# Paged attention of a decoder step: page gathers gated apart, transposes inside the scores, four slots of turned pages

## The chip, the cores and the metric

One Trainium2 chip, of which the program uses one core. The metric is the device time of one execution in microseconds (us). The kernel before takes 3054.34 us, the median of three runs (3053.44 to 3055.99).

## What is computed

The program runs two layers of a decoder on 1024 prompt tokens and on 8 sequences of 8 new tokens. The change touches one stage of the first layer: attention of the new tokens over a cache of pages. Each of the 8 sequences has 64 pages of 128 cached tokens, in an order that a table gives; a cached token is a latent row of 256 numbers (ckv) and a rotary row of 32 (kpe). All in float32.

```python
def mla_scores(q_lat, q_pe, ckv, kpe):
    s = jnp.einsum('bhsr,btr->bhst', q_lat, ckv) + jnp.einsum('bhsk,btk->bhst', q_pe, kpe)
    return s.astype(jnp.float32) * SCALE_B

def online_update(carry, sc, v):
    m, l, acc = carry
    m_new = jnp.maximum(m, jnp.max(sc, axis=-1))
    alpha = jnp.exp(m - m_new)
    p = jnp.exp(sc - m_new[..., None])
    l_new = l * alpha + jnp.sum(p, axis=-1)
    acc_new = acc * alpha[..., None] + jnp.einsum('bhst,btr->bhsr', p, v.astype(jnp.float32))
    return (m_new, l_new, acc_new)

    def page_step(carry, pages):          # of paged_attend
        ck = cache_ckv[layer, pages]
        kp = cache_kpe[layer, pages]
        return online_update(carry, mla_scores(q_lat, q_pe, ck, kp), ck), None
```

## The kernel before

The stage (stage_paged) takes the sequences in four pairs. A pair's tokens are read in 8 units, so there are H = 32 units, which this text calls periods: period h is the work on unit h. One unit is two gathers of 1 MiB, one for each sequence of the pair (e = 0, 1; 128 rows of 8 KB, one row to a partition), and holds two groups g = 2h and 2h + 1 of 4 tokens in each partition. Five sets of buffers hold gathered pages. The rotary rows come in gathers of 256 KB, one for each sequence and two units. All these gathers are issued by GpSimd (gather_pages, L2691; gather_kpe, L2697). Before unit h may be gathered, GpSimd waits until the scores of h - 3 are finished (`scored`) and until the old pages of its set were used (`valued`). It then issues e = 0, e = 1, and in every even period both rotary gathers behind them.

VectorE turns each group by 32x32 blocks (turn_pages, L2701, two of 128x1024 a group; turn_kpe, L2704, two of 128x128) into cT and kT, which have three slots; group g + 3 may only be turned when the scores that read group g are over.

TensorE does for each period, in this order:

- turn_p(h - 1), L3177: 8 transposes of the probabilities of the period before, 128x128, into two PSUM banks;
- scores(h), L3165: 72 matmuls on 32x64 parts of the array (8 chunks of 32 latent numbers and one chunk of rotary numbers, 8 matmuls each), 256 columns, into PSUM S_;
- values(h - 1), L3193: 16 matmuls of 128x64, the turned probabilities by the pages.

In the trace a float32 matmul of scores or values stands as two instructions (144 and 32 a period), a transpose as one (8), and each has a weight load beside it: 184 MATMUL and 184 LDWEIGHTS a period.

After scores(h) VectorE takes the maximum (L3289, L3291, L3293), ScalarE takes the exponential (L3249, L3252), which overwrites the probabilities `pr` and so waits for turn_p(h - 1), and later copies the turned probabilities out of PSUM (copy_p, L3243), for which values(h - 1) waits. VectorE's list for period h is: maxes(h), turn(2h + 3), sums(h - 1) (L3300, L3304), turn(2h + 4). All semaphores and the order on each engine are written out by hand. scores(h) waits for both turned groups, for both turned rotary groups and for the exponential of h - 1 (S_ is one buffer).

SyncE loads the queries of the next pair three times in the stage (load_rows, L2710).

Of the kernel before, what the change touches and what calls it, by code (L numbers as in the profile page):

```python
# [21 lines left out]
F32 = mybir.dt.float32  # L22
# [4 lines left out]
P = 128  # L27
# [9 lines left out]
NH, NOPE, ROPE, VD = 8, 64, 32, 64  # L37
QR, KR = 384, 256
# [2614 lines left out]
class FirstPages:  # L2653
# [3 lines left out]
    def __init__(self, c, cm):  # L2657
        nc = c.nc
        n = 2 * G4 * KR
        self.second = tile(nc, cm, "pages_ckv0", [P, 2 * G4, KR])  # L2660
        raw = nc.alloc_sbuf_tensor_at(f"pages_first_{nc.next_id()}", [P, 2 * G4, KR], F32, offset=c.raw_at)
        self.queries = tile(nc, cm, "q_all", [P, NH * T])
        self.units = [[raw[:, :, :], self.second[:, :, :]]]
        self.units += [[self.queries[:, (2 * u + e) * n:(2 * u + e + 1) * n].rearrange("p (j r) -> p j r", r=KR) for e in range(2)]
                       for u in range(2)]
        self.kpe = tile(nc, cm, "pages_kpe0", [P, 2, NG // NQK, G4 * ROPE])
        m = NG // NQK * G4 * ROPE
        self.later_kpe = self.queries[:, 4 * n:4 * n + m].rearrange("p (a d) -> p a d", a=NG // NQK)
        self.q_rows = tile(nc, cm, "q_rows0", [P, KR // 32 + 1, 2, NH * NT])
        self.keys = tile(nc, cm, "k_all", [P, NH * NPR])  # L2670
        self.own_m = tile(nc, cm, "own_max", [P, NPAIR])
        self.own_b = tile(nc, cm, "own_bias", [P, NPAIR])
        self.sums = tile(nc, cm, "sum_all", [P, NPAIR])
        self.units_in = [nc.alloc_semaphore(f"pages_in{u}") for u in range(2)]
        self.kpe_in = nc.alloc_semaphore("first_kpe_in")
        self.q_in = nc.alloc_semaphore("first_q_in")
        self.turned = nc.alloc_semaphore("pages_turned")
        self.kturned = nc.alloc_semaphore("kpe_turned")
        self.sems = [*self.units_in, self.kpe_in, self.q_in, self.turned, self.kturned]
        n = 3 * 2 * G4 * KR  # L2680
        self.cT = self.keys[:, 0:n].rearrange("p (s e j r) -> p s e j r", s=3, e=2, j=G4)
        m = n + 3 * 2 * G4 * ROPE
        self.kT = self.keys[:, n:m].rearrange("p (s e j r) -> p s e j r", s=3, e=2, j=G4)
        self.later_rows = self.keys[:, m:m + (KR // 32 + 1) * 2 * NH * NT].rearrange("p (n e r) -> p n e r", e=2, r=NH * NT)
# [15 lines left out]
    def turn_pages(self, dve, g, e, src):  # L2700
        return dve.transpose(self.cT[:, g % 3, e, :, :].rearrange("p j r -> p (j r)"), src.rearrange("p j r -> p (j r)"))  # L2701

    def turn_kpe(self, dve, g, e, src):
        return dve.transpose(self.kT[:, g % 3, e, :, :].rearrange("p j r -> p (j r)"), src[e][:, g % (NG // NQK), :])  # L2704

# [347 lines left out]
def stage_paged(c, ckv, ctok, qlat, qpe, yb, ring, w_next, first):  # L3053
# [10 lines left out]
    W = 2 * G4 * P  # L3064
    NCH = KR // 32
    with Stage(nc) as cm:
        last = tile(nc, cm, "pages_ckv1", [P, 2, 2 * G4, KR])
        spare = nc.alloc_sbuf_tensor_at(f"pages_ckv2_{nc.next_id()}", [P, 2, 2 * G4, KR], F32, offset=c.ring_at + 4 * 4 * KD * P)
        units = first.units + [[t[:, e, :, :] for e in range(2)] for t in (last, spare)]
        pk = [[first.kpe[:, 0, :, :], first.kpe[:, 1, :, :]],  # L3070
              [first.later_kpe, tile(nc, cm, "pages_kpe1", [P, NG // NQK, G4 * ROPE])[:, :, :]]]
        cT, kT = first.cT, first.kT
        q9 = [first.q_rows, first.later_rows]
# [4 lines left out]
        ls, own_m = first.sums, first.own_m  # L3078
        wkv = cT[:, 0, :, :, :].rearrange("p e j r -> p (e j r)").rearrange("p (k n) -> p k n", k=2)
        olat = pr.rearrange("p (k h b t) -> p k h b t", k=2, h=NH, b=NB)  # L3080
# [8 lines left out]
        wkv_in, = sems(nc, cm, "wkv_in")  # L3089
        pt_half, = sems(nc, cm, "pt_half")  # L3090
        (own_turned, own_copied, own_valued, own_ready,
# [38 lines left out]
        def _(pool):  # L3130
            for h in range(2, H):
                if h >= 3:
                    pool.wait_ge(scored, h - 2)
                if h >= NSETS:
                    pool.wait_ge(valued, 2 * (h - NSETS) + 2)
                for e in range(2):
                    first.gather_pages(pool, c, units[h % NSETS][e], h, e, p_in[h % NSETS])
                if h % 2 == 0:
                    v = h // 2
                    if v >= 2:  # L3140
                        pool.wait_ge(kturned, (v - 1) * (NG // NQK))
                    for e in range(2):
                        first.gather_kpe(pool, c, pk[v % 2][e], v, e, k_in[v % 2])
# [6 lines left out]
        def _(pe):  # L3150
            def scores(h):
                i = h // NH_
                lo, hi = sorted((2 * h % 3, (2 * h + 1) % 3))
                pair = slice(lo, hi + 1, hi - lo)
                pe.wait_ge(q_in[i % 2], 272 * (i // 2) + 272)
                pe.wait_ge(turned, 2 * h + 2)
                pe.wait_ge(kturned, 2 * h + 2)
                if h >= 1:
                    pe.wait_ge(exped, h)
                for n in range(NCH + 1):  # L3160
                    for a in range(4):
                        rows = slice(32 * a, 32 * a + 32)
                        for e in range(2):
                            keys = cT[rows, pair, e, :, 32 * n:32 * n + 32] if n < NCH else kT[rows, pair, e, :, :]
                            ins = pe.matmul(S_[64 * e:64 * e + 64, a, :].rearrange("p (s j i) -> p s j i", s=2, j=G4),  # L3165
                                            q9[i % 2][rows, n, e, :], keys, start=(n == 0), stop=(n == NCH))
                ins.then_inc(scored, 1)

# [11 lines left out]
            def values(h):  # L3180
# [8 lines left out]
                for j in range(2 * G4):  # L3189
                    g = 2 * h + j // G4  # L3190
                    m = P * (j if 2 * h % 3 < (2 * h + 1) % 3 else (j + G4) % (2 * G4))
                    for e in range(2):
# [14 lines left out]
            for h in range(1, H):  # L3207
                turn_p(h - 1)
                scores(h)
                values(h - 1)  # L3210
# [58 lines left out]
        def _(dve):  # L3269
            def turn(g):  # L3270
                v = g // (NG // NQK)
                if g >= 3:
                    dve.wait_ge(scored, (g - 3) // 2 + 1)
                if g % 2 == 0:
# [31 lines left out]

            turn(2)
            for h in range(H):
                maxes(h)
                if 2 * h + 3 < G:  # L3310
                    turn(2 * h + 3)
                if h == 0:
                    dve.wait_ge(own_valued, 1)
                    for i in range(NPAIR):
                        ins = dve.tensor_copy(acc[:, i, :], ownO[i])
                    ins.then_inc(own_ready, 1)
                else:
                    sums(h - 1)
                if 2 * h + 4 < G:
                    turn(2 * h + 4)  # L3320
            def normalise(lo, hi, done):
# [947 lines left out]
```

## Time and profile before

| what | value |
|---|---|
| median of the runs | 3054.34 us (3053.44 to 3055.99, n = 3) |
| the profiled execution, its own time | 3060.39 us |
| its span | 3058.6 us, 1.8 us less than its time |
| mean granted TensorE clock | 0.967 |
| busy share of TensorE, VectorE, ScalarE, GpSimd | 93%, 57%, 35%, 40% |
| the paged stage, first scores to last values | about 603 to 950 us of the span |

A line of the lists by group gives the busy time in us, then the mean ns of one, then the idle time of the engine just before instructions of the group with what ended it; "issue" is an engine that waited for nothing that the profile shows. A line of the windows gives first the window and its length; the first of them runs from the exponential of period 0 to that of period 31, the others are single periods. A timeline line gives start and duration in us, engine, source line, operation, tiles and shapes, a count where neighbours are merged, and in brackets the idle time before it.

### The profile page before, as it was taken

Reading aid. Unit: us, or ns where it says so; the run is one execution under the profiler, and the core shown is the slowest. Engines: PE = TensorE matmul, PEld = TensorE weight load, DVE = VectorE, ACT = ScalarE, POOL = GpSimd, SP = SyncE. Lnnn points to the kernel's source line nnn. Section 1 sums busy time; section 2 is a strip of 40 time slices with the busy share of each in tenths; the row PEclk is TensorE's granted clock in tenths of the full one; section 3 lists DMA queues with packets and bytes.
Section 4 is the critical chain, followed back from the end, with each engine's and each line's share of the span. In section 5 each row is a group of like instructions: output and inputs, shape, how many; then the busy total and the mean of one; then the engine's idle time right before and its main releaser. Section 6 shows DMA issues by size and latency. Waiting matters only on the chain. (4 is left out here: it accounts for less than half of the span.)

```text
span 3058.6 us, 60317 instructions
## 1 busy us (share of the span) xinstructions
PE 2833.5 (93%) x24873; PEld 2580.9 (84%) x24873; DVE 1741.8 (57%) x3025; ACT 1080.1 (35%) x2174; POOL 1214.7 (40%) x835
## 2 busy tenths in 40 slices
PE   6999899888987989999999997987998999999996
PEld 4888676566666989999999986977998999999996
DVE  5331245566765586666653256888387666664234
ACT  5511026522223553333321034765453333331112
POOL 2411147622223544444433134875544444443202
PEclk8999989999998999999999998999999999999998
DMA  9555300166663322232265232201432232346422
GB/s 313 174 194 191 116 22 1 60 226 229 233 222 94 102 80 100 89 111 99 102 230 186 73 123 76 65 17 31 120 96 85 87 113 88 114 159 214 144 81 81
DMA packets 232380, 377.88 MB, mean 124 GB/s; under 512 B 14506, under 2 KB 155179, under 8 KB 223652
## 3 DMA queue, kind: packets, MB, share of 16 engines
q1 hardware_dynamic: 200092, 253.95, 25.3%
q0 software_dynamic: 11776, 75.50, 6.8%
q10 hardware_dynamic: 20240, 44.57, 4.0%
q8 instruction: 199, 3.26, 0.4%
q14 instruction: 73, 0.60, 0.1%
HBM read 298.71 MB, written 73.28 MB: 122 GB/s over the span
## 5 line engine op out<-in xcount | busy, mean ns | idle before, releaser
L796 PE MATMUL ps<-HS,w_split 128*128 128x272 f32 x1920 | 272.2, 292 | 22.6 <-ACT sg L1053 10.3
L796 PEld LDWEIGHTS ps<-HS,w_split 128*128 128x128 f32 x1920 | 252.9, 190 | 28.3 <-ACT sg L1053 15.0
L812 PE MATMUL ps<-HS,w_ring 128*128 128x272 f32 x1920 | 273.0, 288 | 0.0
L812 PEld LDWEIGHTS ps<-HS,w_ring 128*128 128x128 f32 x1920 | 253.7, 189 | 0.0
L2317 PEld LDWEIGHTS ps<-HS_in,w_split 128*128 128x128 f32 x1728 | 222.6, 191 | 27.7 <-issue 16.4
L2317 PE MATMUL ps<-HS_in,w_split 128*128 128x272 f32 x1728 | 233.4, 294 | 9.2 <-DVE HS_in L2536 9.1
L1791 DVE TENSOR_TENSOR Y<-Y,ps 128x272 f32<-128x272 f32 x256 | 112.2, 438 | 224.6 <-PE ps L812 224.6
L1389 POOL TENSOR_TENSOR w_split<-w_raw,w_split 128x512 fp32r<-128x512 f32 x120 | 170.5, 1433 | 156.0 <-ACT w_split L1045 156.0
L767 PE MATMUL ps<-HS,w_ring 128*128 128x272 f32 x1344 | 179.0, 294 | 22.3 <-PEq L161 12.1
L767 PEld LDWEIGHTS ps<-HS,w_ring 128*128 128x128 f32 x1344 | 174.6, 192 | 24.9 <-POOLq L1438 12.3
L1389 POOL TENSOR_TENSOR w_ring<-w_raw,w_ring 128x512 fp32r<-128x512 f32 x40 | 61.6, 1539 | 269.9 <-ACT w_ring L1045 269.9
L3564 PE MATMUL ps<-HS,w_ring 128*128 128x272 f32 x1032 | 139.5, 298 | 14.6 <-ACT Y L3738 9.0
L3564 PEld LDWEIGHTS ps<-HS,w_ring 128*128 128x128 f32 x1032 | 136.6, 196 | 16.2 <-ACT Y L3738 9.2
L1389 POOL TENSOR_TENSOR hid<-w_raw,hid 128x512 fp32r<-128x512 f32 x80 | 105.2, 1335 | 90.1 <-ACT hid L1045 90.1
L796 PE MATMUL ps<-HS,w_ring 128*128 128x272 f32 x960 | 135.0, 290 | 4.6 <-DVE sg L1657 4.6
L796 PE MATMUL ps<-w_ring,w_split 128*128 128x272 f32 x960 | 135.3, 290 | 0.8 <-DVE sg L1657 0.8
L1385 POOL TENSOR_TENSOR Y<-Y,x_part 128x544 f32<-128x544 f32 x54 | 84.8, 1576 | 129.0 <-DVE Y L1525 107.4
L796 PE MATMUL ps<-HS,hid 128*128 128x272 f32 x960 | 133.4, 288 | 0.5 <-DVE sg L1621 0.5
L796 PEld LDWEIGHTS ps<-HS,w_ring 128*128 128x128 f32 x960 | 127.0, 190 | 5.0 <-DVE sg L1657 5.0
L796 PEld LDWEIGHTS ps<-w_ring,w_split 128*128 128x128 f32 x960 | 127.2, 191 | 1.2 <-DVE sg L1657 1.2
L812 PE MATMUL ps<-HS,w_split 128*128 128x272 f32 x768 | 127.3, 302 | 0.0
L796 PEld LDWEIGHTS ps<-HS,hid 128*128 128x128 f32 x960 | 125.2, 188 | 0.8 <-DVE sg L1621 0.7
(496 smaller groups left out, 6429.0 us busy)
## 6 DMA issues: line engine op xcount, KB each, us to landing
hid_spill<-hid SPq DMA_DIRECT2D x40, 1088.0 KB, 7.3
w_mod_half<-w_mod_in SPq DMA_DIRECT2D x40, 1024.0 KB, 6.2
HS<-hid_spill ACTq DMA_DIRECT2D x32, 1088.0 KB, 11.4
w_raw<-w_ffn_gate_in SPq DMA_DIRECT2D x44, 512.0 KB, 6.4
w_raw<-w_ffn_up_in SPq DMA_DIRECT2D x44, 512.0 KB, 6.1
w_raw<-w_ffn_down_in SPq DMA_DIRECT2D x44, 512.0 KB
x_part<-x_spill SPq DMA_DIRECT2D x54, 272.0 KB, 2.8
x_spill<-Y SPq DMA_DIRECT2D x12, 1088.0 KB, 5.8
```

The source lines that it names most:

```text
L767: ins = pe.matmul(bank(n), wt[:, a, k, :], HS[:, e, k, qs(q)], start=(k == 0 and j == 0), stop=(k == KD - 1 and j == 2))
L796: ins = pe.matmul(psum(U.banks(u)[b]), part_slot(j, a)[:, k, :], token_part(n, j, e)[:, k, :], start=(j < 3 and k == 0 and i == 0), stop=( ...
L812: ins = pe.matmul(down_bank(n), slots[DOWN_SLOT[t]][:, a, d * P:(d + 1) * P], hid_cols(k, t, q)[:, e, :], start=(t == lo and j == 0), stop ...
L1385: pool.tensor_tensor(y, y, xc[:, 2 * (i % 2):2 * (i % 2) + 2, :], ALU.add).then_inc(x_added[p], 1)
L1389: pool.tensor_tensor(part_slot(j, 1), part_from(j), part_slot(j, 0).bitcast(F32), ALU.subtract).then_inc(part_lo, 1)
L1791: dve.tensor_tensor(Y[:, d, qs(q)], Y[:, d, qs(q)], down_bank(n), ALU.add).then_inc(freed, 1)
L2317: ins = pe.matmul(bank(n), wt[:, a, k, :], HS[:, e, k, qs(q)], start=(k == 0 and j == 0), stop=(k == KD - 1 and j == 2))
L3564: ins = pe.matmul(bank(n)[:, 0:Q], weights(slot(t), a, k), HS[:, e, k, qs(q)], start=(k == 0 and i == 0), stop=(k == KD - 1 and i == 2))
```

## The change

- The gather of e = 0 of unit h waits for a new semaphore, `half_scored`, raised when the fifth of the nine chunks of scores(h - 3) is done; the gather of e = 1 waits for `scored` of the same period, as both did before.
- One rotary gather follows the page gathers in each period, where two followed in every second one (unit 2 keeps two; from there odd units issue e = 0 of the next pair of units, even ones e = 1).
- turn_p(h - 1) stands inside scores(h), between its fifth and sixth chunk. The wait for the turned rotary group stands before the ninth chunk instead of at the start.
- Turned pages have four slots in place of three: the pairs of groups of even units in the old buffer, those of odd units in a new one at the start of the ring. The rotary slots are four too. Both groups of a unit lie side by side, so values no longer swaps halves.
- VectorE's list for period h becomes: maxes(h), turn(2h + 4), turn(2h + 5), sums(h - 1), with turn(2) and turn(3) ahead of the loop.

```diff
         self.sems = [*self.units_in, self.kpe_in, self.q_in, self.turned, self.kturned]
-        n = 3 * 2 * G4 * KR
-        self.cT = self.keys[:, 0:n].rearrange("p (s e j r) -> p s e j r", s=3, e=2, j=G4)
-        m = n + 3 * 2 * G4 * ROPE
-        self.kT = self.keys[:, n:m].rearrange("p (s e j r) -> p s e j r", s=3, e=2, j=G4)
+        n = 2 * 2 * G4 * KR
+        self.cT = [self.keys[:, 0:n].rearrange("p (s e j r) -> p s e j r", s=2, e=2, j=G4)]
+        m = n + 4 * 2 * G4 * ROPE
+        self.kT = self.keys[:, n:m].rearrange("p (s e j r) -> p s e j r", s=4, e=2, j=G4)
         self.later_rows = self.keys[:, m:m + (KR // 32 + 1) * 2 * NH * NT].rearrange("p (n e r) -> p n e r", e=2, r=NH * NT)
...
     def turn_pages(self, dve, g, e, src):
-        return dve.transpose(self.cT[:, g % 3, e, :, :].rearrange("p j r -> p (j r)"), src.rearrange("p j r -> p (j r)"))
+        return dve.transpose(self.cT[g // 2 % 2][:, g % 2, e, :, :].rearrange("p j r -> p (j r)"), src.rearrange("p j r -> p (j r)"))
 
     def turn_kpe(self, dve, g, e, src):
-        return dve.transpose(self.kT[:, g % 3, e, :, :].rearrange("p j r -> p (j r)"), src[e][:, g % (NG // NQK), :])
+        return dve.transpose(self.kT[:, g % 4, e, :, :].rearrange("p j r -> p (j r)"), src[e][:, g % (NG // NQK), :])
 
...
     NCH = KR // 32
+    MID = 5
     with Stage(nc) as cm:
...
               [first.later_kpe, tile(nc, cm, "pages_kpe1", [P, NG // NQK, G4 * ROPE])[:, :, :]]]
+        odd = nc.alloc_sbuf_tensor_at(f"k_odd_{nc.next_id()}", [P, 2, 2, G4, KR], F32, offset=c.ring_at)
+        first.cT.append(odd[:, :, :, :, :])
         cT, kT = first.cT, first.kT
...
                 if h >= 3:
-                    pool.wait_ge(scored, h - 2)
+                    pool.wait_ge(half_scored, h - 2)
                 if h >= NSETS:
                     pool.wait_ge(valued, 2 * (h - NSETS) + 2)
-                for e in range(2):
-                    first.gather_pages(pool, c, units[h % NSETS][e], h, e, p_in[h % NSETS])
-                if h % 2 == 0:
-                    v = h // 2
-                    if v >= 2:
-                        pool.wait_ge(kturned, (v - 1) * (NG // NQK))
-                    for e in range(2):
+                first.gather_pages(pool, c, units[h % NSETS][0], h, 0, p_in[h % NSETS])
+                if h >= 3:
+                    pool.wait_ge(scored, h - 2)
+                first.gather_pages(pool, c, units[h % NSETS][1], h, 1, p_in[h % NSETS])
+                for v, e in (((1, 0), (1, 1)) if h == 2 else (((h + 1) // 2, (h + 1) % 2),)):
+                    if v < NPAIR * NQK:
+                        if v >= 2:
+                            pool.wait_ge(kturned, (v - 1) * (NG // NQK))
                         first.gather_kpe(pool, c, pk[v % 2][e], v, e, k_in[v % 2])
...
             def scores(h):
-                i = h // NH_
-                lo, hi = sorted((2 * h % 3, (2 * h + 1) % 3))
-                pair = slice(lo, hi + 1, hi - lo)
+                i, u = h // NH_, h % 2
                 pe.wait_ge(q_in[i % 2], 272 * (i // 2) + 272)
                 pe.wait_ge(turned, 2 * h + 2)
-                pe.wait_ge(kturned, 2 * h + 2)
                 if h >= 1:
...
                 for n in range(NCH + 1):
+                    if n == MID and h >= 1:
+                        turn_p(h - 1)
+                    if n == NCH:
+                        pe.wait_ge(kturned, 2 * h + 2)
                     for a in range(4):
...
                         for e in range(2):
-                            keys = cT[rows, pair, e, :, 32 * n:32 * n + 32] if n < NCH else kT[rows, pair, e, :, :]
+                            keys = cT[u][rows, :, e, :, 32 * n:32 * n + 32] if n < NCH else kT[rows, 2 * u:2 * u + 2, e, :, :]
                             ins = pe.matmul(S_[64 * e:64 * e + 64, a, :].rearrange("p (s j i) -> p s j i", s=2, j=G4),
                                             q9[i % 2][rows, n, e, :], keys, start=(n == 0), stop=(n == NCH))
+                    if n == MID - 1:
+                        ins.then_inc(half_scored, 1)
                 ins.then_inc(scored, 1)
...
                     g = 2 * h + j // G4
-                    m = P * (j if 2 * h % 3 < (2 * h + 1) % 3 else (j + G4) % (2 * G4))
+                    m = P * j
                     for e in range(2):
...
             for h in range(1, H):
-                turn_p(h - 1)
                 scores(h)
...
                 v = g // (NG // NQK)
-                if g >= 3:
-                    dve.wait_ge(scored, (g - 3) // 2 + 1)
+                if g >= 4:
+                    dve.wait_ge(scored, (g - 4) // 2 + 1)
                 if g % 2 == 0:
...
             turn(2)
+            turn(3)
             for h in range(H):
                 maxes(h)
-                if 2 * h + 3 < G:
-                    turn(2 * h + 3)
                 if h == 0:
...
                     ins.then_inc(own_ready, 1)
-                else:
+                for g in range(2 * h + 4, min(G, 2 * h + 6)):
+                    turn(g)
+                if h >= 1:
                     sums(h - 1)
-                if 2 * h + 4 < G:
-                    turn(2 * h + 4)
             def normalise(lo, hi, done):
...
```

## Rows read from the trace of the kernel before

**Rows 1.** The page: engines; the instruction queue of DMA (packets, MB, share)

```profile
PE 2833.5 (93%) x24873; PEld 2580.9 (84%) x24873; DVE 1741.8 (57%) x3025; ACT 1080.1 (35%) x2174; POOL 1214.7 (40%) x835
...
q8 instruction: 199, 3.26, 0.4%
```

**Rows 2.** Windows: us, busy PE PEld DVE ACT POOL, clock, DMA share, GB/s

```profile
615.98:944.04 328.06, 297.51 (x5700) 213.24 (x5700) 227.25 (x401) 74.90 (x125) 80.65 (x85) 0.96 0.60 214
...
634.32:647.15 12.83, 10.59 (x197) 7.78 (x195) 7.48 (x14) 2.41 (x5) 1.90 (x3) 1.00 0.49 166
...
742.73:751.50 8.77, 8.23 (x179) 6.09 (x177) 7.36 (x14) 2.42 (x5) 1.90 (x3) 1.00 0.66 241
751.50:766.76 15.26, 11.87 (x194) 8.23 (x192) 7.48 (x14) 2.42 (x5) 3.80 (x5) 0.89 0.47 174
...
935.03:944.04 9.01, 9.01 (x188) 6.82 (x186) 4.46 (x9) 2.42 (x5) 0.00 (x0) 1.00 0.08 17
```

**Rows 3.** Groups of TensorE in the stage, 615.98 to 944.04

```profile
L3165 PE MATMUL ps<-k_all 32*64 32x256 f32 x2304 | 77.1, 392 | 14.6 <-issue 14.6
L3193 PE MATMUL ps<-pages_ckv,ckv 128*64 128x256 f32 x490 | 74.0, 402 | 1.7 <-issue 1.7
L3165 PE MATMUL ps<-k_all,q_rows 32*64 32x256 f32 x2160 | 70.6, 384 | 12.8 <-issue 12.6
```

**Rows 4.** Timeline of 764 to 774: one period without a wait

```profile
764.81 3.69 PE L3193 MATMUL ps<-pages_ckv,ckv 128*64 128x256 f32 x32
...
766.76 1.10 ACT L3252 ACTIVATE ckv<-ps,run 128x1024 f32<-128x1024 f32 x1
...
768.43 1.09 PE L3177 MATMUL ps<-cst,ckv 128*128 128x128 f32 x8
...
769.45 4.14 PE L3165 MATMUL ps<-k_all 32*64 32x256 f32 x144
769.55 1.03 ACT L3243 ACTIVATE ckv<-ps 128x1024 f32<-128x1024 f32 x1 [1.60 <-PE ps L3177]
```

**Rows 5.** Timeline of 632 to 644: a period with waits

```profile
632.71 0.95 POOL L2691 DMA_INDIRECT pages_first<-cache_ckv_in,ckv_rows  x1 [4.84 <-PE ps L3165]
633.88 3.40 PE L3193 MATMUL ps<-q_all,ckv 128*64 128x256 f32 x29 [0.87 <-issue]
633.96 0.95 POOL L2691 DMA_INDIRECT pages_ckv<-cache_ckv_in,ckv_rows  x1 [0.30 <-issue]
638.23 2.83 PE L3165 MATMUL ps<-k_all,q_rows 32*64 32x256 f32 x90
643.30 1.95 PE L3165 MATMUL ps<-k_all,q_rows 32*64 32x256 f32 x54 [2.24 <-issue]
```

**Rows 6.** DMA in 634.3:637.6, 637.6:640.9, then 640.9:642.0, then 644.3:645.5, in 40 slices

```profile
q0 software_dynamic: 108, 0.88, 98.4%
...
q0 software_dynamic: 178, 1.21, 88.0%
...
DMA  0090000000000000000000000000000000000000
...
q8 instruction: 1, 0.02, 5.6%
...
DMA  0009000000000000000000000000000000000000
...
q8 instruction: 1, 0.02, 5.2%
```

**Rows 7.** Timeline of 626 to 629: transposes beside the fourth gather

```profile
626.34 1.09 PE L3177 MATMUL ps<-cst,ckv 128*128 128x128 f32 x8
626.90 0.96 POOL L2697 DMA_INDIRECT pages_kpe<-cache_kpe_in,kpe_rows  x1 [0.30 <-PE ps L3193]
...
628.77 3.66 PE L3165 MATMUL ps<-k_all,q_rows 32*64 32x256 f32 x114 [0.23 <-issue]
628.80 1.03 ACT L3243 ACTIVATE ckv<-ps 128x1024 f32<-128x1024 f32 x1 [2.87 <-PE ps L3177]
```

More of the change, by code:

```diff
@@ L3078, in stage_paged @@
         ls, own_m = first.sums, first.own_m
-        wkv = cT[:, 0, :, :, :].rearrange("p e j r -> p (e j r)").rearrange("p (k n) -> p k n", k=2)
+        wkv = cT[0][:, 0, :, :, :].rearrange("p e j r -> p (e j r)").rearrange("p (k n) -> p k n", k=2)
         olat = pr.rearrange("p (k h b t) -> p k h b t", k=2, h=NH, b=NB)
@@ L3089, in stage_paged @@
         wkv_in, = sems(nc, cm, "wkv_in")
-        pt_half, = sems(nc, cm, "pt_half")
+        pt_half, half_scored = sems(nc, cm, "pt_half", "half_scored")
         (own_turned, own_copied, own_valued, own_ready,
```

## The prediction

> **What bounds the kernel now.** I read the page first: TensorE is busy 93% of the span and leads the chain that ended last, so only TensorE's time counts. Then I cut the paged stage into windows from one exponential (L3252) to the next. 31 periods take 328.06 us, 10.58 each; the quickest take 8.77, others up to 15.26 [rows 2]. The quick period is TensorE alone: values start at 764.81, transposes at 768.43, scores at 769.45 and end at 773.59, 8.78 us with no gap [rows 4]. So 31 x 8.77 = 271.9 us is the floor of this order and 56.2 us lie above it. That is the purse; the rest of the kernel is untouched.
>
> Where the 56.2 us are: the groups of TensorE show 14.6 + 12.6 + 1.7 = 28.9 us idle with the releaser "issue", thus no semaphore [rows 3]. The granted clock is 0.96 over the stage; if the missing 0.04 is time at the lower level of 1.2 GHz, 8% of 328 us ran at half pace and lost 13 us [rows 2]. The third share is a hold-up beside a rotary gather, below.
>
> What "issue" hides is seen in one period [rows 5, 6]. Values stop at 633.0 for 0.87 us, scores stop after 90 of 144 for 2.24 us and go on at 643.30. Through 634.3 to 640.9 the DMA shows only the software queue, the two page gathers, 0.88 + 1.21 MB. At 640.98 a packet of the instruction queue appears, some 1.0 us long; TensorE goes on 1.3 us after its end. The next such packet starts at 644.4, 1.1 us after scores resumed, with DMA idle. So this is TensorE's code: the page has 199 such packets, 3.26 MB, 16.4 KB each, for 49,746 matrix instructions, about 250 in each [rows 1]. Whenever TensorE enters a block of code the next block is asked for; with DMA free it is usable after 1.1 + 1.0 + 1.3 = 3.4 us; behind gathers it comes when their stretch ends, here 7.1 us after TensorE resumed at 633.88. A block is about 127 of a period's 184 matmul records (the rest of the 256 are loads and waits); inside scores it is used up in 127/144 x 4.14 = 3.65 us [rows 4].
>
> The Trainium skill, Advanced Engine Details and Errata, ISA Cache, gives lines of 16 KB, 256 instructions; the trace agrees with its 250 matrix instructions plus waits.
>
> **The gathers.** *Gated apart.* Call the end of scores 0. Now gather A is issued at +0.2, B 1.25 us later, DMA starts about 1.6 us after A's issue, and the stretch runs 6.6 us (3.3 us a gather) to about +8.4; with both rotary gathers it is over a microsecond longer [rows 5, 6]. A block boundary early in it starves until then, and the code is usable at +8.4 + 2.3 = +10.7, in the next period. After the change A is issued when five of nine chunks are done. Between that and the end of scores lie the transposes (1.02) and four chunks (4/9 x 4.14 = 1.84), 2.9 us; with a change of array shape 3.05. A moves bytes from about -1.2 to +2.1, B from +1.8 to +5.1, the one rotary gather (0.26 MB) to about +5.7.
>
> *What the code does then.* TensorE's period runs: values 0 to 3.7, five chunks to 6.0, transposes to 7.0, four chunks to 8.8. Boundaries advance by 127 of 184 records, so of three in a row (2.07 periods) one falls in the last four chunks, the next in the first five or the transposes, the next in values or close by. (a) Boundary at -1.8 to 0: the request comes while A alone is in the queue. Let in at A's end, at most +2.2, the code is usable at +4.5; the next boundary comes at +4.4 to +7.2: wait 0 to 0.1. (b) Boundary in values, request under B: let in at +5.7, usable at +8.0; next boundary at +7.3 to +8.5: 0.35 on average. (c) Boundary in the first chunks: DMA is free, no wait. Transposes inside scores help too: a block inside scores now lasts 119/144 x 4.14 + 1.02 = 4.4 us instead of 3.65, above the 3.4 us. Sum: 15 triples x 0.5 = 8 us, with slow clock after waits 9 us. Bounds: 0, if every request is let in; all of the present waits, if none is (a rival).
>
> The Trainium skill, DMA: Bandwidth & Descriptors, Queues, rings and completion order, has each engine alternate between queues a packet at a time. By it a fetch would never wait for two gathers, but the one asked for at 633.88 did [rows 5, 6], so I don't build on it; were it true, (a) would hold all the more.
>
> *One rotary gather a period.* GpSimd issues as many in all, 0.96 us each, and has more than 4 us idle a period. But in one period the transposes began at 626.34, the fourth gather was issued at 626.90, and the copy that needs the transposes began at 628.80, not 2.78 us after the exponential as in a free period but 4.06; scores hitched too [rows 4, 7]. I count about ten periods of 9.6 us or so without a long wait, +0.8 each, 8 us. With one rotary gather, issued 1.5 us after scores and thus in values, where A and B cost nothing now, this goes. Bounds: 0 to 8 us gained.
>
> **Transposes within scores.** The same 8 instructions. The array changes shape four times a period instead of three. Starts lie 1.02 us apart for 8 transposes and 0.30 us at the turn to transposes where neighbours lie 0.1 to 0.2 apart, so one change more costs 0.2 us: 6 us in all; bounds 0 and 0.4 a period, 12 us. The Trainium skill, TensorEngine Tiling (Array Packing), Key Properties, says that a change of tiling mode drains the engine; it speaks against this edit, and the 0.2 us is how the trace prices it. The copy of the turned probabilities (1.03 us) was covered by 4.14 us of scores, now by 1.84: 0.7 us spare [rows 4]. If that is gone, it costs what is missing. The exponential still ends before values do; scores wait for it as before.
>
> **Four slots and VectorE's order.** VectorE works 7.4 us of 8.77 a period [rows 2]; the same work stays. Today group 2h + 3 is turned only after scores(h), 4.5 us behind their end, while the next scores start at 4.7: with transposes moved they would start at 3.7 and be late; with four slots both groups are there a period ahead. Pages are now wanted at +1.5 of the following period instead of later, but land by +5.7 before it, 4.6 us spare. Sums come at +7.4 to +8.1; the values that need their buffer are a period later. The values' halves no longer swap: nothing. The last chunk's own wait: nothing. SyncE's loads: unchanged. The odd buffer lies where the ring is filled only after the last scores but one's values: nothing. At the head, unit 3's first gather lengthens the first stretch by 3.3 us; the code then fetched has over 5 us to spare today: 0.
>
> **Sum.** 56.2 above the floor now; after: code 9 + change of shape 6 + other 1 = 16. Gain 40 us, less 1 for the head: 39 us. From the profiled execution's own 3060.39 that is 3021.4; that execution was 6.05 above the median of 3054.34, so 3015.3.
>
> **Rivals.**
> - *Starved anyway* (0.17): A lasts 3.3 us and B follows 3.05 us behind it, so the stretch is one and case (a) waits until +5.0, code usable at +7.4: 1.8 us on average, with (b) 2.1 x 15 = 32, slow clock 12, shape 6: 50 against 56.2, gain 6: 3048. For it: today's fetches are let in only at the end of the stretch, though one request preceded B's bytes. Against: B's first bytes come only when A is all but through.
> - *Slower: one seamless stretch with the rotary gather in it* (0.10): the same place, but the fetch is let in at the end of all three, +6.3 if each takes its full time, usable at +8.6. Case (a) waits 3.0, (b) 0.7: 3.7 x 15 = 55, less what alignment spares (today's pattern reckoned this way overstates by a third) 38, clock 17, shape 12: 67, 11 us more than now: 3066. It decides once the end lies later than about +5.9.
> - *The gather holds up the transposes* (0.12): gather A is issued just ahead of transposes, in every period. If it does what the fourth gather did, 0.87 us each [rows 7], 27 us go: 3042. Against: in the first scores the first two gathers stopped nothing.
> - *Something else is late*, DVE or a page, and eats the rest (0.03).
>
> **Chances and range.** Forecast 0.58, its own range 3002 to 3030 (bounds of code, shape and rotary terms). No cost and no wait at all gives 3054 - 56 = 2998. The range 3000 to 3054 takes in the forecast, the hold-up and most of starved anyway. 0.2% is 6 us, about what a measurement of this kernel tells from no change: faster 0.58 + 0.12 + half of 0.17, taken as 0.77; slower 0.11; same 0.12.
>
> **What would show it.** Right: periods mostly 8.9 to 9.5, none above 12; "issue" idle of scores and values under 10 us; granted clock near 1.00 in the stage; instruction packets between A's and B's bytes; transposes 8 in 1.1 us with ScalarE's copy at once behind; 0.2 us more at turns. Wrong: scores stopping 2 to 3 us among the first five chunks once in two periods (starved); a copy over a microsecond behind the last transpose (hold-up); values beginning late behind the copy, or scores behind VectorE's turns.

## The result, and the profile after

The changed kernel takes 3004.58 us (median of 4 runs, 3002.60 to 3010.64) against 3054.49 us for the kernel before (4 runs): a ratio of 0.9838, 95% interval 0.9825 to 0.985. It is faster by 49.9 us; the forecast was 39 (3015, range 3000 to 3054). The profiled execution took 3005.89 us, 54.5 less than that of before. Of these 54.5 us, 49.0 lie in the 31 periods, 3.2 ahead of them, where nothing was changed (the first scores begin at 599.78 us instead of 602.94), and 2.3 elsewhere.

The page of the changed kernel, engines and instruction queue, answers to [rows 1]:

```profile
PE 2811.7 (94%) x24873; PEld 2556.3 (85%) x24873; DVE 1730.8 (58%) x3025; ACT 1078.7 (36%) x2174; POOL 1217.3 (41%) x835
...
q8 instruction: 199, 3.26, 0.4%
```

Its windows, columns as in [rows 2]: the stage from the first exponential to the last, the first two periods, an ordinary one, and the worst of the later ones:

```profile
612.86:891.95 279.09, 277.63 (x5700) 191.13 (x5700) 223.56 (x397) 74.77 (x125) 79.52 (x84) 1.00 0.72 250
...
612.86:622.92 10.06, 10.06 (x190) 7.17 (x190) 8.37 (x16) 2.40 (x5) 3.47 (x4) 1.00 0.92 323
622.92:631.52 8.60, 7.67 (x174) 5.52 (x172) 7.32 (x14) 2.38 (x5) 2.21 (x3) 1.00 0.65 240
631.52:640.40 8.88, 8.88 (x186) 6.13 (x184) 7.35 (x14) 2.41 (x5) 2.85 (x4) 1.00 0.77 268
684.68:694.66 9.98, 9.51 (x188) 6.25 (x186) 7.37 (x14) 2.43 (x5) 2.87 (x4) 1.00 0.82 282
```

The same instructions (5700) now take 279.09 us instead of 328.06, at a clock of 1.00 instead of 0.96, so TensorE stays at 2.4 GHz. Its groups in the stage, as [rows 3]:

```profile
L3200 PE MATMUL ps<-pages_ckv,ckv 128*64 128x256 f32 x490 | 68.5, 382 | 0.0
L3170 PE MATMUL ps<-k_all 32*64 32x256 f32 x1280 | 41.4, 379 | 0.5 <-issue 0.5
L3170 PE MATMUL ps<-k_all,q_rows 32*64 32x256 f32 x1136 | 36.7, 379 | 1.0 <-ACT ckv L3258 0.9
L3170 PE MATMUL ps<-k_odd,k_all 32*64 32x256 f32 x1024 | 32.3, 381 | 0.0
```

The idle time of scores and values put down to "issue" is 0.5 us now. Before it was 28.9 us in the three groups of [rows 3], and 30.3 with a fourth one of values, which the prediction left out:

```profile
L3193 PE MATMUL ps<-q_all,ckv 128*64 128x256 f32 x384 | 46.2, 390 | 1.4 <-issue 1.4
```

The timeline of the kernel after shows a period without a wait and the worst of the later ones (answers to [rows 4, 5]):

```profile
677.57 2.41 PE L3170 MATMUL ps<-k_all 32*64 32x256 f32 x80
679.91 1.09 PE L3184 MATMUL ps<-cst,ckv 128*128 128x128 f32 x8
680.93 1.98 PE L3170 MATMUL ps<-k_all 32*64 32x256 f32 x64
682.85 3.67 PE L3200 MATMUL ps<-q_all,ckv 128*64 128x256 f32 x32
686.45 2.41 PE L3170 MATMUL ps<-k_odd,k_all 32*64 32x256 f32 x80
688.79 1.09 PE L3184 MATMUL ps<-cst,ckv 128*128 128x128 f32 x8
689.82 1.55 PE L3170 MATMUL ps<-k_odd,k_all 32*64 32x256 f32 x48
691.16 0.59 PE L3170 MATMUL ps<-k_all 32*64 32x256 f32 x2
692.22 0.69 PE L3170 MATMUL ps<-k_all 32*64 32x256 f32 x14 [0.47 <-issue]
```

From start to start: scores 2.34, transposes 1.02, scores 1.92, values 3.60, together 8.88 us. Scores alone now take 4.26 us instead of 4.14. The one wait stands 50 of 64 into the second part of scores.

### The profile page after: what moved, and what is told of

Read it like the earlier page. It is cut to its first block and busy times, and to the rows that moved or that the text cites. A ratio compares the mean times of both kernels' runs of the same rounds, so it can differ in the third digit from the quotient of the medians.

```text
span 3004.1 us, 60286 instructions
## 1 busy us (share of the span) xinstructions
PE 2811.7 (94%) x24873; PEld 2556.3 (85%) x24873; DVE 1730.8 (58%) x3025; ACT 1078.7 (36%) x2174; POOL 1217.3 (41%) x835
```

## The experiments

The first eight ran on a chip on which the kernel before takes 3043.7 us (3043.5 for the second four), the last four on one where it takes 3055.6, so ratios are each to the runs of before on the same chip. "Stage" is the window from the first exponential to the last of the profiled execution, as above; it is the finer measure. No profile of the kernel before was taken on these two chips. The times that I expected were set against a kernel before of 3054 us, some 11 us more than on the first chip, so there it is the distance to before that compares with them.

| run | edit | us | ratio to before, 95% | stage, us |
|---|---|---|---|---|
| e1_both_at_end | after, both page gathers wait for the end of scores | 3023.77 | 0.9937 (0.9916 to 0.9957) | 303.60 |
| e2_both_at_half | after, both wait for the fifth chunk | 3002.17 | 0.9865 (0.984 to 0.989) | 279.26 |
| e3_two_rotary | after, two rotary gathers in even periods | 3005.32 | 0.9872 (0.9849 to 0.9895) | 278.02 |
| e4_transposes_ahead | after, transposes ahead of scores again | 2996.43 | 0.9847 (0.9824 to 0.987) | 275.36 |
| e5_before_apart_short | before, first gather after the fifth chunk | 3014.72 | 0.992 (0.9888 to 0.9952) | 293.13 |
| e6_before_apart_long | before, first gather after the second chunk | 3002.07 | 0.9877 (0.9846 to 0.9908) | 278.11 |
| e7_before_few_rotary | before, rotary gathers left out from the third on | 3040.53 | 0.9997 (0.9983 to 1.0012) | 324.37 |
| e8_head | after, VectorE's turn(4) ahead of the copies of period 0 | 3006.63 | 0.9887 (0.9856 to 0.9918) | 279.34 |
| e9_apart_late | after, gathers at the end of scores and of values | 3052.11 | 0.9988 (0.9977 to 0.9998) | 324.53 |
| e10_after_again | after, unchanged | 3008.93 | 0.9844 (0.9827 to 0.9862) | 278.73 |
| e11_ahead_two_rotary | e4 with two rotary gathers in even periods | 3020.30 | 0.9883 (0.9867 to 0.99) | 288.95 |
| e12_ahead_both_early | e4, both gathers after the second chunk | 3112.30 | 1.0191 (1.0173 to 1.021) | 378.87 |

**Distance or early start.** e1 and e2 take the distance away (the two gathers are issued 1.25 us apart), once at the late place and once at the early one.

```diff
-                    pool.wait_ge(half_scored, h - 2)    # e1: both wait for scored
+                    pool.wait_ge(scored, h - 2)
...
-                if h >= 3:                              # e2: both wait for half_scored
-                    pool.wait_ge(scored, h - 2)
```

> The changed kernel, but both page gathers of a period wait for the end of the scores, 1.25 us apart, as before; all else as changed. Theory (the gathers' spacing decides when TensorE's code comes): A, B and the rotary gather are one stretch from about +1.8 to +9 us behind the scores, a code request made under it is let in at its end, one wait of some 3 us in two periods, 15 x 3 plus slow clock: 3040 to 3055 us. Rival (transposes inside the scores and four slots carry the gain): at most 3012 us.

> The changed kernel, but both page gathers wait for the fifth chunk of the scores, 1.25 us apart. It has the early start without the spacing. Theory (spacing): the code request made in the last chunks starves to the end of the stretch at about +6 us, wait some 2.5 us in the first chunks of the next scores once in two periods: 3035 to 3055 us. Rival (it is the early start that counts, the stretch being over sooner): 3003 to 3012 us.

e2 is as good as the changed kernel: 279.26 us against 279.09 in the first comparison and 279.34 for e8 below, whose edit changed next to nothing, on this same chip. e1 loses 24.5 us of the stage. It takes 20 us less than the kernel before on its chip, where my two ranges meant 14 at most and 42 at least, so both of them missed: a late start costs a good part of the gain, but not all of it. With late gathers, then, the other parts of the change save some 20 us together. Which of them does was not taken apart. What is lost in e1 are stops of scores, as in [rows 5] but shorter, about once in two periods. The timeline of e1:

```profile
652.01 1.09 PE L3184 MATMUL ps<-cst,ckv 128*128 128x128 f32 x8
653.04 1.09 PE L3170 MATMUL ps<-k_odd,q_rows 32*64 32x256 f32 x24
655.37 0.88 PE L3170 MATMUL ps<-k_odd,q_rows 32*64 32x256 f32 x20 [1.25 <-issue]
```

and its DMA in 652.9 to 654.1, in which the packet of the instruction queue appears:

```profile
DMA  0986909998090909669970990096096699699903
...
q0 software_dynamic: 54, 0.40, 90.1%
q8 instruction: 1, 0.02, 4.8%
```

The packet comes in the midst of the second gather's bytes, not at its end. That the stops are those of the code can be counted: from the end of one stop to the end of the next TensorE runs 381 matmul records, three times the 127 of the prediction. Two windows of e1:

```profile
635.30:655.37 20.07, 18.82 (x381) 12.95 (x381) 14.70 (x26) 4.82 (x8) 5.69 (x6) 1.00 0.66 235
...
675.34:695.73 20.39, 18.82 (x381) 12.76 (x381) 14.70 (x26) 4.82 (x8) 5.68 (x6) 1.00 0.80 263
```

So on this chip the early start is needed and the distance is not.

**The one edit on the kernel before.** e5 and e6 leave all else of before and release the first gather early: 1.73 and 3.02 us ahead of the second.

```diff
-                    pool.wait_ge(scored, h - 2)
+                    pool.wait_ge(half_scored, h - 2)
...
                 for e in range(2):
+                    if h >= 3 and e == 1:
+                        pool.wait_ge(scored, h - 2)
                     first.gather_pages(pool, c, units[h % NSETS][e], h, e, p_in[h % NSETS])
...
+                    if n == 4:                          # e6: n == 1
+                        ins.then_inc(half_scored, 1)
```

> The kernel before with nothing but the first page gather released after the fifth chunk of the scores, the second at their end: about 1.9 to 2.1 us between them, two rotary gathers behind in even periods. Theory (a gap between the gathers' bytes is needed, a gather takes 3.3 us): little is gained, 3035 to 3055 us. Rival (any earlier start helps): 3015 to 3030 us.

> The kernel before with nothing but the first page gather released after two of the nine chunks: about 3.3 us between the gathers. Theory (spacing alone gives most of the gain): 3010 to 3025 us, with the hold-ups beside the fourth gather left in, some 8 us. Rival (it takes the whole change): 3040 us or more.

e6 takes 278.11 us in the stage, as the changed kernel does: this one wait brings all of it (41 us less than before, within what I had expected). e5, with the gather 1.3 us later, has 15 us more, with single stops of up to 3.9 us.

In these four runs the stage follows the time at which the first gather is issued, counted from the start of values: 0.4 us behind it in e1 (646.48 against 646.07) for 303.60 us, 1.3 ahead in e5 (651.93 against 653.25) for 293.13, 2.5 ahead in e2 (727.27 against 729.79) for 279.26, and 2.6 ahead in e6 (643.48 against 646.10) for 278.11.

**The other parts.**

```diff
-                for v, e in (((1, 0), (1, 1)) if h == 2 else (((h + 1) // 2, (h + 1) % 2),)):
+                for v, e in ((h // 2, 0), (h // 2, 1)) if h % 2 == 0 else ():        # e3
...
-                    if n == MID and h >= 1:                                          # e4
-                        turn_p(h - 1)
...
-                    if n == MID - 1:
+                    if n == 1:
...
             for h in range(1, H):
+                turn_p(h - 1)
                 scores(h)
...
-                    for e in range(2):                                               # e7, on before
+                    for e in range(2 if v < 2 else 0):
...
-                dve.wait_ge(k_in[v % 2], 32 * (v // 2) + 32)
+                dve.wait_ge(k_in[v % 2], 32)
...
                 if h == 0:                                                           # e8
+                    turn(4)
                     dve.wait_ge(own_valued, 1)
...
-                for g in range(2 * h + 4, min(G, 2 * h + 6)):
+                for g in range(2 * h + 4 if h else 5, min(G, 2 * h + 6)):
```

> The changed kernel, but with two rotary gathers in every even period and none in odd ones. Theory (a fourth gather in a row holds TensorE up when transposes or scores run beside it; here it is issued 2.7 us behind the scores, so its effect falls on the end of values and the start of scores): 0 to 0.9 us in 15 periods, 3004 to 3018 us. Rival (one rotary gather a period is worth nothing): 3004 us within 3.

> The changed kernel, but the transposes stand ahead of the scores again, and the first gather is released after two of the nine chunks, which keeps about 3.2 us between the gathers. Theory (spacing is what counts): one change of array shape less, 0.11 us a period, against blocks of code that are used up inside scores in 3.65 us instead of 4.4: 2998 to 3012 us. Rival (the transposes inside the scores are needed, since they stretch the shortest block): 3018 us or more.

> The kernel before, with the rotary gathers left out from the third pair of units on, so that later units use the rotary rows of the first ones (the output is not the reference's). Theory (the fourth gather of an even period holds the transposes and scores up by 0.8 us where they stand beside it, and lengthens the stretch by a microsecond): 8 to 20 us less than before, 3034 to 3046 us, and no period of 9.6 us without a stop in it. Rival (the 9.6 us periods have another cause): they stay, and the time falls by what shorter stretches save only.

> The changed kernel, but in period 0 VectorE turns one group before it copies the new tokens' own values out of PSUM, and the other after. In the changed kernel the copies wait for TensorE, so the two turns and the next maximum come late and TensorE stands 1.3 us before scores(2). Theory: about 1 us less, 3003 to 3004 us.

e3: one rotary gather a period is worth nothing by itself on this chip (278.02 us with two). e4: with the transposes ahead of scores, and the first gather released after the second chunk so that it is as early, the stage takes 3.7 us less, most periods 8.70 us:

```profile
717.42:726.12 8.70, 8.70 (x188) 6.33 (x186) 7.35 (x14) 2.41 (x5) 2.86 (x4) 1.00 0.80 275
```

Beside an early start, then, standing within scores costs the transposes something and brings nothing. e7 leaves out 256 KB gathers, so its later scores lack new rotary rows: the periods of 9.6 us without a stop for code are gone, but the stops for code are as long as before and the time is the same (ratio 0.9997), where I had expected 8 to 20 us less: on this chip the rotary gathers cost nothing. e8 missed as well: turn(4) ahead of the copies waits for its own page.

```profile
614.26 2.37 DVE L2701 STREAM_TRANSPOSE k_all<-q_all 128x1024 f32<-128x1024 f32 x2 [2.36 <-DMA q_all<-cache_ckv_in,ckv_rows]
```

**A late start with distance, and three more.**

```diff
-                    pool.wait_ge(half_scored, h - 2)     # e9: first gather
+                    pool.wait_ge(scored, h - 2)
...
-                    pool.wait_ge(scored, h - 2)          # e9: second gather
+                    pool.wait_ge(valued, 2 * h - 6)
```

> After, but the first gather of a unit waits for the end of scores and the second for the end of the values that follow them: the two are issued 3.6 us apart as in the changed kernel, or a little more, but both about 3 us later. Both gathers at the end of scores gave 303.6 us for the 31 periods, both at the half 279.25, the changed kernel 279.10. My prediction's theory (a fetch of code asked for while the first gather is queued alone is let in at that gather's end, so distance is what helps): clearly better than both at the end, 31 periods at 280 to 293 us. The theory that holds after these runs (what counts is when the stretch of both gathers lies against the boundaries of the code, and it must begin before the end of scores): distance doesn't replace the early start, the stretch now reaches into the next scores, 31 periods at 300 us or more, and the time not under that of both at the end (ratio to before 0.99 to 1.00).

> The changed kernel as it is, on the chip of the experiments, where the kernel before takes 3043 us: both theories say the same, 31 periods within 1 us of 279.1 and a ratio of 0.985 to 0.988, as for the same kernel with two rotary gathers or with both gathers at the half. It is there as the measure for the others.

> After, with the transposes ahead of scores again (the first gather released after the second chunk, so that it starts as early) and both rotary gathers in even periods: the two edits that were each a little better than the changed kernel, together. If what they save is separate (0.18 us a period for one change of shape less, and one stop less), 31 periods at 274 to 275.5 us, about 4 to 5 us under the changed kernel. If the rotary gathers behind the early page gathers again lie beside the transposes, and hold them up as in the kernel before, some periods of 9.5 us come back and the 31 take 278 to 284 us.

> After, with the transposes ahead of scores again and both gathers released after the second chunk, 1.25 us apart. If only the early start counts, this is as good as the same with the second gather at the end of scores (31 periods 275.4 us, here 274 to 277). If distance counts where scores last only 4.1 us without the transposes in them (a block of code inside them 3.65 us against a fetch of 3.4), waits of 0.5 to 2 us come back at the boundaries in values and in the first chunks: 31 periods at 280 to 290 us.

These four ran on the second chip, e10 too, which was meant as the measure of the first; its 278.73 us are within my range. e9's numbers fell where the second theory put them, but for another reason, so it decides nothing between the two; for that it would have to run on the first chip, and it did not. Its periods are nearly all 10.7 us long, with stops at the same matmuls of scores each time, while a boundary of the code moves by 127 of 184 records a period. Two windows from one exponential to the next, then the timeline of GpSimd, then of TensorE's weight loads in the same scores:

```profile
667.72:678.41 10.69, 10.46 (x188) 6.40 (x186) 7.35 (x14) 2.41 (x5) 2.85 (x3) 1.00 0.64 224
...
678.41:689.11 10.70, 10.49 (x188) 6.43 (x186) 7.38 (x14) 2.44 (x6) 2.84 (x3) 1.00 0.67 225
```

```profile
669.65 0.95 POOL L2691 DMA_INDIRECT pages_ckv<-cache_ckv_in,ckv_rows  x1 [2.60 <-PE ps L3200]
670.90 0.96 POOL L2697 DMA_INDIRECT pages_kpe<-cache_kpe_in,kpe_rows  x1 [0.30 <-issue]
```

```profile
669.30 1.09 PEld L3170 LDWEIGHTS ps<-k_all,q_rows 32*64 32x64 f32 x47 [0.39 <-issue]
670.95 0.22 PEld L3170 LDWEIGHTS ps<-k_all,q_rows 32*64 32x64 f32 x5 [0.57 <-issue]
671.67 0.22 PEld L3170 LDWEIGHTS ps<-k_all,q_rows 32*64 32x64 f32 x5 [0.50 <-issue]
672.40 0.66 PEld L3170 LDWEIGHTS ps<-k_all,q_rows 32*64 32x64 f32 x23 [0.51 <-issue]
```

GpSimd issues a page gather and the rotary gather while scores run. From 670.39, 0.74 us after the start of the first issue, TensorE gets five loads and their matmuls every 0.72 us, where scores otherwise take one pair in 0.029 (4.14 us by 144); the full pace is back at 672.40, 0.54 us after the end of the last issue. I call each such halt among the loads, here three, a step. In e12 three gathers are issued beside scores, at 851.69, 852.93 and 854.18, and its loads show five steps:

```profile
850.22 2.35 PEld L3166 LDWEIGHTS ps<-k_odd,q_rows 32*64 32x64 f32 x85 [0.17 <-issue]
853.00 0.20 PEld L3166 LDWEIGHTS ps<-k_odd,q_rows 32*64 32x64 f32 x3 [0.43 <-issue]
853.72 0.22 PEld L3166 LDWEIGHTS ps<-k_odd,q_rows 32*64 32x64 f32 x6 [0.51 <-issue]
854.45 0.20 PEld L3166 LDWEIGHTS ps<-k_odd,q_rows 32*64 32x64 f32 x5 [0.51 <-issue]
855.16 0.20 PEld L3166 LDWEIGHTS ps<-k_odd,q_rows 32*64 32x64 f32 x3 [0.51 <-issue]
855.89 0.47 PEld L3166 LDWEIGHTS ps<-k_odd,q_rows 32*64 32x64 f32 x21 [0.53 <-issue]
```

e12 ends up 1.9% slower than the kernel before. e11, with one gather beside scores and one step in each period that has gathers (9.36 us nearly all of them), ends up behind the changed kernel. Both missed what I expected, e12 by 89 us.

The changed kernel itself gives 278.73 us on this chip. Its second and third gather are issued beside values, which ask for one load and matmul in 0.11 us (32 in 3.60), less often than scores in a step (5 in 0.72). Its first gather is issued beside transposes, but that alone doesn't explain why it is spared. In e11 the loads stop 0.87 us after the start of the issue (707.05 against 706.18). In e10 the first gather of a period is issued at 703.25. By that lag a step would come at 704.12, when scores go on already, and there is none: 64 loads in 1.53 us. The loads, e11 first, then e10:

```profile
704.71 2.34 PEld L3168 LDWEIGHTS ps<-k_all 32*64 32x64 f32 x83 [0.17 <-issue]
707.49 1.60 PEld L3168 LDWEIGHTS ps<-k_all 32*64 32x64 f32 x61 [0.43 <-issue]
```

```profile
703.86 1.53 PEld L3170 LDWEIGHTS ps<-k_all 32*64 32x64 f32 x64 [0.17 <-issue]
```

The hold-up of [rows 7] in the kernel before looks like the same thing. Its loads of scores stand still for 0.68 us and go on 0.91 us after the end of the fourth issue (627.86), and ten of the 31 periods have such a halt, all of them with two rotary gathers. That it is the same is not shown:

```profile
627.39 0.69 PEld L3165 LDWEIGHTS ps<-k_all,q_rows 32*64 32x64 f32 x30 [0.20 <-issue]
...
628.77 2.34 PEld L3165 LDWEIGHTS ps<-k_all,q_rows 32*64 32x64 f32 x89 [0.68 <-issue]
```

But the chip matters too. In e6, on the first chip, a gather is issued at the same place in scores as in e11, and nothing stops; its loads and GpSimd's issue:

```profile
641.99 3.72 PEld L3167 LDWEIGHTS ps<-k_all,q_rows 32*64 32x64 f32 x144 [0.22 <-issue]
```

```profile
643.48 0.95 POOL L2691 DMA_INDIRECT q_all<-cache_ckv_in,ckv_rows  x1 [2.28 <-PE ps L3167]
```

e4 is the same. e6 has the same order as e11 on TensorE and GpSimd, and differs in the slots of turned pages, VectorE's list and the place of one wait. No kernel with such steps ran with a profile on both chips, so whether the chip or a detail of the order decides stays open. Two things speak for the chip: the kernel before takes 12 us less on the one where no step was seen, of the order of what its ten hold-ups cost (some 8), and e7 shows that the rotary gathers cost nothing there. e2, too, ran only there. It issues its second gather beside scores, so on a chip with steps the distance may yet be worth having; that is untested.

## Why the prediction was right, and where not

The total came out 11 us better than forecast, the terms as follows: code 2.9 us and not 9, transposes 3.4 and not 6, other 0 and not 1, the head 0.9 and not 1, and some 1 us outside of them. The largest term was right in sign for a reason that the runs don't bear out, which is luck: the edit that was to put a distance between the gathers also starts the first one earlier.

**What bounds, and the purse.** Right: 56.2 us above the floor of 271.9 were there to be had, and 49.0 were. 7.2 are left: 31 x 0.11 = 3.4 for the longer periods, 0.9 at the head (10.06 and 8.60 against twice 8.88), and 2.9 of waits, 1.1 of them in the period of 9.98.

**The gathers.** The size was off in the good direction: 2.9 us of waits where I had put 9. At first sight the picture of case (a) is to be seen. In the changed kernel a gather is issued at 644.78 and the next at 647.72. These are its DMA windows from 645.0 to 649.4, then to 650.6:

```profile
q0 software_dynamic: 127, 1.03, 69.4%
...
q0 software_dynamic: 45, 0.25, 84.8%
q8 instruction: 1, 0.02, 4.7%
```

1.03 MB is the first gather, and the packet stands right behind it. But counted back from the stop at 692.22 by seven blocks of 127 records, TensorE entered the block only at about 649.3, in values and not in the last chunks of scores as case (a) has it, when the first gather was all but over. So this fetch had hardly anything to wait for:

```profile
649.30:692.20 42.90, 42.45 (x890) 29.25 (x887) 35.02 (x62) 11.89 (x20) 13.00 (x14) 1.00 0.82 276
```

A true case (a) is the next one. TensorE entered the block at about 655.2 (six blocks, 762 records, ahead of the same stop), in the last chunks, with the gather issued at 653.67 alone in the queue. The packet comes at 656.86, in the midst of that gather and not at its end; the second is issued at 656.61. These are the windows 654 to 656.85 and 656.85 to 657.9:

```profile
q0 software_dynamic: 46, 0.37, 49.8%
...
q0 software_dynamic: 57, 0.47, 108.3%
q8 instruction: 1, 0.02, 5.2%
```

So a fetch needs no end of a gather to be let in. The step "A lasts 3.3 us, B comes 3.05 behind, so a fetch is let in between" names the wrong cause for the gain: e2 has no such space and loses nothing. What e1, e2, e5 and e6 show in its place is that the gain follows the time at which the stretch begins, 2.5 us ahead of values or more. Why a fetch gets by sooner then stays open: no run takes by itself what decides how long a fetch waits among the bytes of gathers. In e1 one came after 1.55 MB, here one after 0.37 MB. e9 could not say whether distance would help a late start, since its stops have another cause.

**Slow clock.** Right: 0.96 rose to 1.00, with the waits gone.

**One rotary gather a period.** The hold-up of [rows 7] is gone, as forecast. Whether by the number of rotary gathers or by the place of their issue (beside values now), e3 can't say, though it has two of them and no hold-up: it ran on the chip where e5 and e6, with two as well, show no such period either, where e7 gains nothing by leaving them out, and where the kernel before is faster by 11 us from the start. For the place speaks e11, on a chip with steps: it issues two rotary gathers in every second period, beside values, and its periods are nearly all 9.36 us long, with them and without. The 8 us that I gave the term are not confirmed by a run that changes it alone on such a chip.

**Transposes within scores.** The period is 8.88 us against 8.77, which makes 3.4 us where I had put 6. But the edit by itself costs what I had put: e4, which has the rest of the change and one change of shape less, runs at 8.70, so it is 0.18 us a period, 5.6 us in all, against 0.2 and 6. The Trainium skill, TensorEngine Tiling (Array Packing), Key Properties, says that changing the tiling mode drains TensorE; e4 agrees in sign. What was wrong is a term that I had put at nothing. With three changes of shape as in the kernel before, e4 is 0.07 us a period faster, 2 us in all: its scores take 4.08 us (702.63 to 706.71) instead of 4.14. That comes with the slots or VectorE's list; which, and why, was not tested. As a cure for starved code the edit is not shown. e1 has it and saves 20 us with late gathers, but it has the slots too, and it still takes 24.5 us more than the changed kernel.

**The head.** 1 us forecast, 0.9 measured, by another way than I gave: VectorE has both turns of period 0 to do behind the copies, the maximum of period 1 begins at 621.12, and TensorE waits 0.93 us for the exponential.

**The rivals.** Starved anyway, and one seamless stretch: no stop above 1.1 us, so neither. Gather A holds up the transposes: ScalarE's copy begins within 0.1 us of the end of the transposes (843.08 behind 841.95 + 1.09), in e10 too (703.97 behind 702.84 + 1.09); not here. But its idea, that issuing a gather disturbs TensorE, came true in e9, e11 and e12, where the gather lies beside scores. I had looked for it beside the transposes alone.

**The best version.** e4 is the fastest that ran, 2996.43 us, 5.7 below e2 on the same chip. It issues a gather within scores, as e11 does, which has steps on the other chip; until e4 has run there, the changed kernel is the safer one.

## What to carry to other kernels

When an engine idles for "issue" with a heavy software queue beside it, look for packets of the instruction queue and move the start of the transfers earlier against the stretch where instructions are used fastest; one wait moved (e6) did what the whole change did. Then look at where GpSimd issues: beside the 128x64 matmuls of values it cost nothing in these runs, beside the short ones of scores it stopped TensorE again and again on one chip and not on another. So compare on one chip only, and try a placement on more than one. Compare the mechanism with the parts taken one by one, since a right total (and e9's right number) can come from a wrong cause.

## What was unexpected of the hardware

While GpSimd issues gathers beside scores, TensorE can fall to some five loads with their matmuls in 0.72 us, from 0.7 to 0.9 us after the start of the first issue (0.74 in e9, 0.87 in e11, 0.88 in e12) to 0.4 to 0.8 us after the end of the last (0.54, 0.37 and 0.75). One issue brought one step, two brought three, three brought five. With three gathers at that place e12's periods are 3.3 us longer on average than e4's on the other chip (378.87 and 275.36 by 31), in part by a lower clock (0.94), and the kernel is slower than before. One gather at the same place cost nothing in e4 and e6 on another chip. And the kernel before takes 3043.5 or 3055.6 us by the chip, while the changed one varies less (3004.58 in the first comparison, 3006.63 for e8, whose edit changed next to nothing, and 3008.93 for e10).
